# Order of the last down products of a feed-forward, grain of the first norm steps, and order of the weight loads behind them

## The reference, cut to what matters

```python
def _swiglu(h, w_gu, w_down):
    gate, up = jnp.split(h @ w_gu, 2, axis=-1)
    return (jax.nn.silu(gate) * up) @ w_down
...
x = _layer_norm(alpha * x + 0.5 * _swiglu(x, ffn_w_gu[l, 0], ffn_w_down[l, 0]), ln_g[l, 0], ln_b[l, 0])
```

## Time and profile before

| | |
|---|---|
| median of 3 runs | 1468.13 us (1465.68 to 1469.3) |
| the profiled execution | 1464.74 us |
| its span, first to last instruction | 1463.1 us |
| mean granted TensorE clock, as a share of full | 0.963 |
| PE busy | 94% of the span |
| DVE busy | 63% |
| ACT busy | 50% |
| the chain that ended last | PE 74%, DVE 14%, ACT 7%, DMA 3% |
| DMA | 229.17 MB, mean 157 GB/s |
| ACT idle until down rows have landed | 67.2 us in 45 waits, the longest 3.6 us |

### The profile page before, as it was taken

One profiled execution on the slowest core, in us unless ns is written; L12 is line 12 of the kernel. 1 busy time (PEld: TensorE's weight loads), 2 busy tenths in 40 slices (PEclk: granted clock), 3 DMA queues, 4 the chain that ended last, 5 costly groups with the idle time before them and its releaser, 6 DMA issues.

```text
span 1463.1 us, 20466 instructions
## 1 busy us (share of the span) xinstructions
PE 1379.1 (94%) x8222; PEld 1211.8 (83%) x8222; DVE 920.1 (63%) x1343; ACT 726.1 (50%) x1141; POOL 92.6 (6%) x137
## 2 busy tenths in 40 slices
PE   6899799998899999998899999899999999899997
PEld 6788788887788888987888888788888888888886
DVE  3787666776765666636665656756568446666656
ACT  5556355555455553545255555455553545355452
POOL 1233000000000000500000000000001400000000
PEclk9798899999999998999899999999999999899999
DMA  7223366666476563330566566475654331375561
GB/s 226 87 90 128 87 203 200 188 199 196 118 230 199 173 189 106 116 116 30 149 187 202 188 199 186 153 209 173 200 164 145 104 116 50 114 235 179 181 201 50
DMA packets 301191, 229.17 MB, mean 157 GB/s; under 512 B 13083, under 2 KB 283818, under 8 KB 301098
## 3 DMA queue, kind: packets, MB, share of 16 engines
q1 hardware_dynamic: 301082, 227.88, 51.2%
q10 hardware_dynamic: 16, 0.00, 0.0%
HBM read 226.80 MB, written 1.05 MB: 156 GB/s over the span
## 4 chain that ended last, share of the span: by engine, by line
PE 74%; DVE 14%; ACT 7%; DMA 3%; issue 1%; POOL 0%; SPq 0%; ACTq 0%; DVEq 0%
PE bank L855 20%; PE bank L783 11%; PE bank L784 11%; PE bank L785 11%; PE bank L858 10%; DVE lo_gu L1630 5%; ACT hi_gu L1292 4%; PE bank L1198 2%; PE bank L1168 2%; PE bank L985 2%; DVE lo_dn L1635 1%; DMA st_dn<-in_ffn_w_down 1%; DVE conv L1782 1%; PE bank L1178 1%; DVE stats L1657 1%
## 5 line engine op out<-in xcount | busy, mean ns | idle before, releaser
L855 PE MATMUL bank<-xT,hi_gu 128*128 128x512 f32 x1616 | 405.8, 393 | 4.8 <-DVE lo_gu L1630 4.0
L1630 DVE TENSOR_TENSOR lo_gu<-st_gu,hi_gu 128x2048 fp32r<-128x2048 f32 (+2 forms) x146 | 323.9, 2221 | 122.6 <-ACT hi_gu L1292 122.6
L855 PEld LDWEIGHTS bank<-xT,hi_gu 128*128 128x128 f32 x1616 | 297.5, 189 | 64.4 <-DVE lo_gu L1630 6.2
L1292 ACT ACTIVATE hi_gu<-st_gu 128x2048 fp32r<-128x2048 f32 (+3 forms) x147 | 270.4, 1843 | 18.5 <-PE bank L785 10.1
L858 PEld LDWEIGHTS bank<-xT,lo_gu 128*128 128x128 f32 x1616 | 221.5, 191 | 16.0
L858 PE MATMUL bank<-xT,lo_gu 128*128 128x256 f32 x1616 | 226.1, 283 | 0.0
L783 PE MATMUL bank<-hi_dn,actTh 128*128 128x512 f32 x436 | 172.0, 394 | 6.7 <-DVE actTl L1764 4.4
L784 PE MATMUL bank<-lo_dn,actTh 128*128 128x512 f32 x436 | 170.9, 392 | 0.0
L785 PE MATMUL bank<-hi_dn,actTl 128*128 128x512 f32 x436 | 169.7, 389 | 0.0
L1785 DVE TENSOR_TENSOR act<-act,bank 128x256 f32<-128x256 f32 x101 | 42.5, 421 | 173.2 <-ACT act L1378 173.2
L1299 ACT ACTIVATE hi_dn<-st_dn 128x1024 fp32r<-128x1024 f32 x109 | 114.6, 1056 | 67.2 <-DMA st_dn<-in_ffn_w_down 67.2
(11 more groups left out here) (269 smaller groups left out, 1844.2 us busy)
## 6 DMA issues: line engine op xcount, KB each, us to landing
st_gu<-in_ffn_w_gu SPq DMA_DIRECT2D x176, 512.0 KB, 5.1
st_dn<-in_ffn_w_down SPq DMA_DIRECT2D x109, 512.0 KB, 6.6
st_gu<-in_w_in SPq DMA_DIRECT2D x23, 1024.0 KB, 5.3
st_gu<-in_w_out SPq DMA_DIRECT2D x12, 1024.0 KB, 5.1
st_gu<-in_ffn_w_gate SPq DMA_DIRECT2D x21, 512.0 KB, 3.9
st_gu<-in_ffn_w_val SPq DMA_DIRECT2D x21, 512.0 KB, 5.3
st_gu<-in_w_in SPq DMA_DIRECT2D x10, 512.0 KB, 4.4
gb<-in_ln_g SPq DMA_DIRECT2D x6, 512.0 KB, 7.2
```

The lines of the kernel that those rows point to most:

```text
L855: pe.matmul(b[:, :], hv[:, w, k, :], xT[:, k, :, :].rearrange("p a b -> p (a b)"), start=k == 0, stop=k == KD - 1, skip_group_check=True)
L1292: i = act.activation(high, staged, ACT.Copy)
L1630: i = dve.tensor_tensor(low, staged, high.bitcast(F32), ALU.subtract)
```

## The change

The tail runs by quarters: for each m and each h the four tiles, so `bank[0]` is complete first, then `bank[1]`, `bank[2]` and `bank[3]`, each with a signal of its own (`sum_done[f, m, h]`). The wait for `prod_low` and `dn_low` of a tile stands ahead of its part in the first quarter. In the norms that are not `begun`, DVE takes the statistics of quarter (0, 0) right behind its addition, ahead of the addition of quarter (0, 1). The four waits that meant the whole of a token half name the second quarter of it. SP loads pair and down rows tile by tile. No instruction is added to or taken from PE, ACT or DVE, and no DMA.

```diff
         def wait_summed(eng, i, m, h):
             kind, st = NORMS[i][3]
             if kind == "ffn":
-                eng.wait_ge(sum_done.sem, sum_done[st, m])
+                eng.wait_ge(sum_done.sem, sum_done[st, m, h])
...
             def ffn_loads(f):
-                for j0 in range(2, FFN_TILES[f], 2):
-                    here = range(j0, min(j0 + 2, FFN_TILES[f]))
-                    if j0 == 6:
+                for j in range(2, FFN_TILES[f]):
+                    if j == 6:
...
-                    for j in here:
-                        load_pair(CHUNK_NO["ffn", f, j])
-                    for j in here:
-                        load_down(tile_no(f, j))
+                    load_pair(CHUNK_NO["ffn", f, j])
+                    load_down(tile_no(f, j))
...
-            def down(f, j, m):
+            def down(f, j, m, cols=(0, 1)):
                 g, last = tile_no(f, j), j == FFN_TILES[f] - 1
                 t = g % RING
-                if m == 0:
+                if m == 0 and cols[0] == 0:
                     pe.wait_ge(prod_low.sem, prod_low[g])
                     pe.wait_ge(dn_low.sem, dn_low[g])
-                for h in range(2):
+                for h in cols:
                     hs, ts = slice(h * HALF, (h + 1) * HALF), slice(m * P, (m + 1) * P)
                     i = mm3(bank[2 * m + h][:, :], (actTh[:, t, ts], actTl[:, t, ts]), (hi_dn[t][:, hs], lo_dn[t][:, hs]),
                             j == 0, last, skip_group_check=True)
-                if last:
-                    i.then_inc(sum_done.sem, sum_done.one((f, m)))
-                elif m == 1:
+                    if last:
+                        i.then_inc(sum_done.sem, sum_done.one((f, m, h)))
+                if m == 1 and cols[-1] == 1 and not last:
                     i.then_inc(down_done.sem, down_done.one(g))
...
                 for m in range(M):
-                    for j in tail:
-                        down(f, j, m)
+                    for h in range(2):
+                        for j in tail:
+                            down(f, j, m, (h,))
...
                 for h in range(2):
                     if not (begun and h == 0):
                         add(i, 0, h)
-                for h in range(2):
-                    if not (begun and h == 0):
                         statistics(i, 0, h)
                 variance(i, 0)
```

More of the change, by code:

```diff
@@ L500, in wait_down @@
             if g == FFN_FIRST[f] + FFN_TILES[f] - 1:
-                eng.wait_ge(sum_done.sem, sum_done[f, 1])
+                eng.wait_ge(sum_done.sem, sum_done[f, 1, 1])
             else:
@@ L586, in ffn_loads @@
             def ffn_loads(f):
-                for j0 in range(2, FFN_TILES[f], 2):
-                    here = range(j0, min(j0 + 2, FFN_TILES[f]))
-                    if j0 == 6:
+                for j in range(2, FFN_TILES[f]):
+                    if j == 6:
                         norm_rows({0: 2, 1: 3, 2: 5, 3: 6, 4: 8}[f])
-                    if f == 0 and j0 == 8:
+                    if f == 0 and j == 8:
                         sp.dma_start(staged_distances, C["distances"]).then_inc(bias_loaded.sem, bias_loaded.dma())
-                    if f == 0 and j0 == 12:
+                    if f == 0 and j == 12:
                         sp.dma_start(staged_slopes, C["slopes"]).then_inc(bias_loaded.sem, bias_loaded.dma())
-                    if f == 0 and j0 == 16:
+                    if f == 0 and j == 16:
                         sp.dma_start(rope, C["rope"].rearrange("p m a b -> p m (a b)")).then_inc(bias_loaded.sem, bias_loaded.dma("all"))
                         layer_vectors(0)
-                    for j in here:
-                        load_pair(CHUNK_NO["ffn", f, j])
-                    for j in here:
-                        load_down(tile_no(f, j))
+                    load_pair(CHUNK_NO["ffn", f, j])
+                    load_down(tile_no(f, j))
             def layer_vectors(l):
@@ L1335, in norm @@
                         l = (i - 3) // 3
-                        act.wait_ge(sum_done.sem, sum_done[1 + 2 * l, 1])
+                        act.wait_ge(sum_done.sem, sum_done[1 + 2 * l, 1, 1])
                         weights_high(CHUNK_NO["in2", l, 2])
```

## The result

The changed kernel takes 1473.18 us in the median of 10 runs (1468.77 to 1476.25) against 1467.78 us (10 runs, 1460.67 to 1469.30): ratio 1.0046, 95% interval [1.0027, 1.0065], slower by 5.4 us. The forecast was 1472.5 us. Its profiled execution took 1474.31 us (span 1472.6, mean granted clock 0.959), 9.5 us of span more than the one of before.

A forecast was written before the change was run, and what follows sets the result against it. PE was taken as the bound inside the feed-forwards, leaving the five tails and feed-forward 0. Terms 1.4 + 1.4 + 0.4 - 0.4 + 1.6 = +4.4 us on the 1468.1 us median gave 1472.5 us, range 1466 to 1477.

The forecast's parts named there:

- The stops: PE waits for `actTl` behind each tail's ninth product; +1.4 us each in f = 1 and f = 3.
- f = 2: Tail of f = 2: the same stop, partly taken by PE's wait for DVE's norm ahead of the turn; +0.4 us.
- f = 4 with the end: Last tail to the span's end: earlier additions on DVE against a 0.4 us stop; -0.4 us.
- f = 0: First feed-forward up to its turn: -0.3 us with the loads' gain, +1.9 us of clock loss, together +1.6 us.
- The clock: PE at half clock behind the 3 to 5 us stop of f = 0; 1.9 us lost, bounds 0 and 4.1.
- The loads' 1.0 us: Loads tile by tile remove ACT's waits for down rows, so `actTl` in f = 0 is ready 1.0 us sooner.
- DVE's order: In the norms, each statistic right behind its own addition waits for it: three steps, 0.36 us.
- Pair 3: Tile 3's pair load, queued behind tile 2's down rows at each feed-forward's start; taken as no cost.
- rival 3: More clock loss, from a 1.4 us stop or f = 3's second turn: 1.5 to 5 us more, 1474 to 1477.5; chance 0.18.
- Rival 2: The forecast without clock loss in f = 0: +2.5 us, 1470.6 us; chance 0.14.
- rival 4: Not slower: the 10 us at half clock at 570 us are gone, -5.0 us, 1467.5 or 1465.6; chance 0.14.
- rival 5: Pair 3 arrives late and reaches PE at feed-forward starts, each us costing up to 4 us over four; chance 0.04.

The follow-up runs named there:

- kernel 9: Kernel before with loads tile by tile and the rotary table's load, which releases GpSimd's casts, moved to tile 6 of f = 1; ratio 0.9964.
- 12: Kernel 11 with the rotary table's load, which releases GpSimd's casts, moved to tile 6 of f = 1; ratio 0.9954.
- 3: Changed kernel with the tail's first token half tile by tile, both column halves together, as before; ratio 0.998.
- 11: Changed kernel, tail reordered, DVE's new order only in the last norm, last tile's `weights_low` behind the turned half in f = 0 and 2; ratio 0.9949.
- kernel 6: Kernel before with each DVE statistic right behind its addition, nothing else; ratio 1.0002.
- 2: Changed kernel with the loads by twos again, as before; ratio 1.0057.
- 4: Changed kernel with the last tile second in the first quarter, behind three products instead of nine; ratio 1.009.
- kernel 5: Changed kernel with quarters in the first token half only in f = 0, that half by tiles in f = 1 to 4; ratio 0.9989.
- 8: Kernel before with only the rotary table's load, which releases GpSimd's casts, moved to tile 6 of f = 1; ratio 0.9988.

## Why the prediction held, and where it was off

**The stops** were where it put them and set the result: the earlier trace rows and one multiplication were enough. The term of 1.40 us in f = 1 and f = 3 measured 1.52 and 1.55. The gap of starts is 1.62 - 0.23 = 1.39 us; the first product behind a stop takes 0.34 us instead of 0.23, which I had set at 0.05 for the restart and within the 1.40. f = 2 was +0.32 for +0.4, f = 4 with the end -0.29 for -0.4.

**f = 0** was +1.6 at the first turn, and the turn came at 374.38, +1.87. Two terms in it were off against each other. The clock lost 1.7 us where 1.9 was taken. That this was so near is luck: the trace of before has seven stops of 3.5 us and more behind its first products, not five, and half clock lasted 5.2 to 8.1 us behind each; the 3.8 us of the row at 1210 us are the length of the window, the half clock there went on to 1215.2. The loads' 1.0 us did not come: `actTl` was 5.90 us behind the first product, as before (5.93), and the 0.8 us by which the turn looks earlier were there at the stage's first product, ahead of any change. The step that failed is "a wait of ACT that DVE doesn't share pushes the round a little too", a gain costed without GpSimd in it. With loads tile by tile the two casts meet two instructions of DVE and take 1.6 to 1.8 us of this stage (kernels 9 and 12 against 3 and 11); in the profiled execution of before they stretched one, by 0.67 us. Counted from the stage's first product, f = 0 cost 0.27 + 2.42 = 2.7 us.

**DVE's order** was 0.36 and measured 0.27 at the one turn that waits for it: three dependent steps of 0.09 us, not 0.12. In f = 1 and f = 3 it was to be hidden behind the stop, and kernel 6, without the stop, shows 0.15 there.

**Pair 3** behind the down rows cost nothing: 21.0 us from the turn of f = 0 to f = 1's products as before, and 158.09 inside f = 1.

**The sum.** The tails and the end give 2.42 + 1.52 + 0.32 + 1.55 - 0.29 = 5.5 us, 5.8 with the 0.27; the medians give 5.4. That they meet is partly luck. The profiled pair differs by 9.5 us: 4.84 more lie in the second mixer, at the clock of the window at 1118.8. The forecast counted such a loss as rival 3, chance 0.18, so by its mechanism the profiled execution is rival 3 and not the forecast. Of the profiled executions, the three kernels with a stop in f = 3's tail (changed, 2, 4) all lost 2.6 to 4.9 us there, of the eleven without one only kernel 6 did (3.0). With kernel 5's 8.7 us this speaks for the stop as a cause of it, one execution of each is no proof. In the other direction, all three other kernels with loads by twos (2, 6, 8) have the last tile of f = 0 1.5 us later than the profiled execution of before, and stage 0 takes 188.3 us in 6 and 8, not 185.4: a typical run of before seems to lose about 3 us there, which the tile-by-tile loads save. So I read the 5.4 us as 5.5 of tails, up to 3 back from the loads, and about as much of clock in the second mixer. The first is shown, the split of the rest is argued. One number of all runs bears on it: span x (1 - mean granted clock), the time lost to the clock, is 57.7 us in the mean of the changed kernel's ten runs and 54.2 in 30 runs of the kernel before, taken beside the first experiments. That is 3.5 us more (standard error 1.4), and the rest of the span grew by 2.0 (0.7). The tails without their 1.7 us of clock are 3.8 us longer, so some 1.8 came back elsewhere, which fits the reading of the loads, and clock is the larger part of the slowing in the mean of the runs.

**Rival 2** (no clock loss in f = 0) is refuted by the half clock behind its stop, **rival 4** by the half clock at 573 us, which stayed, **rival 5** by f = 1's length.

## What to carry to other kernels

Ahead of an operand that arrives at a known time, count the products that cover the wait. Sorting a reduction so that one output ends early takes cover from the last-arriving operand, and can cost more at its head than it gives at its end: here it gained 0.3 us where nothing followed and lost 1.5 where it had no slack. Then order the products so that everything that doesn't need the late operand stands ahead of it, and look who is the bound at once afterwards: in f = 0 the wait only moved to DVE until DVE's own late work was moved too.

## What the runs showed of the hardware that was not expected

- An instruction of DVE with two SBUF inputs was stretched by 0.84 us, twice, by casts of 1.51 and 1.23 us on GpSimd, an engine that is busy 6% of the span. In f = 1 two of DVE's were stretched too (2.95 us for 2.29, 1.25 for 0.42), and a cast took 3.11 us. Where two met in these rows, the one that started later waited. Where DVE is near the bound, a small cast on GpSimd belongs where DVE isn't.
- A stop of 1.23 us cost 1.52 in a row of dense products. One of 2.60 us cost 4.5 (15.40 - 10.92), with half clock behind it in three tails of three, and one of 3.58 had 1.7 us of clock loss behind it. Stops of 1.60 to 1.71 us in tails had full clock behind them (five cases), one of 1.80 us half clock (kernel 9).
- The same mixer took 178.2 to 194.4 us in single executions of kernels that don't touch it, at granted clocks of 0.87 to 0.96 over it.
